# Feed-forward gate and up as seven block products, with weight sums by accumulating DMAs

## The chip, the cores and the metric

One Trainium2 chip, of which the kernel uses one core. The metric is the time of one execution on the device in microseconds (us).

## The reference

A sequence of 512 tokens with 1024 features goes through a network of two layers (one with a gated linear recurrence, one with stick-breaking attention), each followed by a feed-forward, and then through a second network with three kinds of attention, gates and an expert feed-forward. What is changed here is the first step of the two feed-forwards of the first network:

```python
def _rmsnorm(x, g):
    y = x32 * lax.rsqrt(jnp.mean(x32 * x32, axis=-1, keepdims=True) + RMS_EPS)
    return (y * g.astype(jnp.float32)).astype(x.dtype)
...
def _swiglu(h, w_gate, w_up, w_down):      # h = _rmsnorm(x, norm_ffn_g[layer])
    g = h @ w_gate.astype(h.dtype)
    u = h @ w_up.astype(h.dtype)
    return (jax.nn.silu(g) * u) @ w_down.astype(h.dtype)
```

w_gate and w_up have 1024 rows and 2816 columns, w_down the reverse.

## The kernel before

Activations lie transposed: X holds eight chunks c of 128 features (partitions) by 512 tokens. Every dense product is float32 work split into rounded parts: an operand is a high part in the rounded type fp32r and a low part, the rest, and the product is high x high, high x low and low x high, three matmuls for each tile of 128 x 128 weights (lines 2241 to 2243 in `pe_tiles`). The name WH, WL stands for a weight's high and low part, HH, HL for those of the normed input, MH, ML for those of the feed-forward's inner activation.

The whole kernel is one list of steps, written out once by `Order` and its callers; each engine's program walks over the same list and takes the steps that concern it, so the list is at once the order of each engine's queue. Engines wait for each other by semaphores. A weight *unit* is 128 output columns by up to eight k tiles (1024 elements for each partition). SP loads the units in order into six buffers RAW (line 1259), and reloads a buffer when DVE has made the low part of its last user (line 1249). Step `split` makes the parts: ACT rounds RAW to WH (line 1386), DVE subtracts to get WL (line 1712). There are three slots for parts; a unit is split two units ahead of its use, when the step of its matmuls is listed (line 125), and ACT waits until the slot's last user is through PE (line 1385).

In a feed-forward (`ffn_order`, line 331) the 2816 inner columns are 22 tiles f of 128, in two halves of eleven. For each f the list has gate's product (unit wg, eight k tiles, 24 matmuls of 512 columns), up's (wu, likewise), and the step `swiglu`: DVE scales both results from PSUM by the token scale RS (line 1722), ACT applies silu (1493), DVE multiplies (1844), ACT rounds the product to MH (1495), DVE makes ML (1716). After each half come eight down products of eleven k tiles (units of six and five) which DVE adds into X (`add_x`, line 1833). RS is 1/sqrt of the mean square; its steps (`rest`) come within the first tile's products, so that the norm's scale by token is applied to the results. The norm's scale by feature is applied ahead: step `high` rounds X times the gain to HH on ACT (1414) and squares X (1418), POOL adds up the squares (1369, 1372), step `low` makes HL on DVE (1752). At the entry of a feed-forward (norms 1 and 3) these steps follow each chunk of the output projection before it; the first tile's matmuls wait chunk by chunk.

## Time and profile before

| | |
|---|---|
| time, median of 3 executions | 2109.82 us (2109.67 to 2110.99) |
| span of the profiled execution, first to last instruction | 2108.2 us |
| clock granted to TensorE, mean | 0.999 |
| instructions | 24868 |
| moved by DMA | 352.09 MB, mean 167 GB/s |

The profile is of one execution; its span is 1.6 us under the median. No other time of that execution is given. A line of grouped instructions has the line of the kernel, the engine, the operation, output and inputs with their shape, the count, then busy time, mean duration and what the engine waited for before them. Durations of neighbouring instructions overlap, so the step between two starts is often shorter than one of them.

### The profile page before, as it was taken

Reading aid. Unit: us, or ns where it says so; the run is one execution under the profiler, and the core shown is the slowest. Engines: PE = TensorE matmul, PEld = TensorE weight load, DVE = VectorE, ACT = ScalarE, POOL = GpSimd, SP = SyncE. Lnnn points to the kernel's source line nnn. Section 1 sums busy time; section 2 is a strip of 40 time slices with the busy share of each in tenths; the row PEclk is TensorE's granted clock in tenths of the full one; section 3 lists DMA queues with packets and bytes.
Section 4 is the critical chain, followed back from the end, with each engine's and each line's share of the span. In section 5 each row is a group of like instructions: output and inputs, shape, how many; then the busy total and the mean of one; then the engine's idle time right before and its main releaser. Section 6 shows DMA issues by size and latency. Waiting matters only on the chain.

```text
span 2108.2 us, 24868 instructions
## 1 busy us (share of the span) xinstructions
PE 2082.8 (99%) x10137; PEld 1514.3 (72%) x10137; DVE 1022.5 (49%) x1516; ACT 749.7 (36%) x1076; POOL 143.7 (7%) x148
## 2 busy tenths in 40 slices
PE   9999999999999999999999999999999999999998
PEld 7878888888777788888888777777788534444433
DVE  7875433444666664434446656554564312122123
ACT  7774322323455543222333556433333110011012
POOL 0220000001000020000001010162100000000000
PEclk9999999999999999999999999999999999999999
DMA  5233223223211133233233322242236999999996
GB/s 220 76 104 110 86 81 124 98 72 116 76 61 60 61 108 100 72 119 102 76 95 111 115 67 72 60 94 73 68 110 247 392 426 427 427 427 426 427 427 273
DMA packets 89808, 352.09 MB, mean 167 GB/s; under 512 B 9568, under 2 KB 24160, under 8 KB 66144
## 3 DMA queue, kind: packets, MB, share of 16 engines
q1 hardware_dynamic: 84720, 342.48, 43.9%
q0 software_dynamic: 2192, 2.63, 1.0%
q10 hardware_dynamic: 2784, 5.41, 0.7%
q8 instruction: 81, 1.33, 0.3%
q14 instruction: 31, 0.25, 0.0%
HBM read 347.06 MB, written 2.10 MB: 166 GB/s over the span
## 4 chain that ended last, share of the span: by engine, by line
PE 87%; DMA 4%; DVE 4%; ACT 3%; issue 1%; POOL 0%; SPq 0%; ACTq 0%; DVEq 0%; POOLq 0%
PE PS L2241 20%; PE PS L2243 20%; PE PS L2242 20%; PE PS L2648 8%; PE PS L2690 4%; DMA SL<-in_wgu_dram 4%; PE PS L2284 2%; PE PS L2358 1%; PE PS L2632 1%; PE PS L2382 1%; PE PS L2372 1%; PE PS L2633 1%; DVE XC L1779 1%; PE PS L2480 1%; DVE WL L1712 1%
## 5 line engine op out<-in xcount | busy, mean ns | idle before, releaser
L2241 PE MATMUL PS<-HH,WH 128*128 128x512 f32 x1392 | 552.9, 397 | 0.8 <-DVE ACC L1942 0.6
L2243 PE MATMUL PS<-HH,WL 128*128 128x512 f32 x1392 | 542.5, 390 | 0.0
L2242 PE MATMUL PS<-HL,WH 128*128 128x512 f32 x1392 | 541.9, 389 | 0.0
L1712 DVE TENSOR_TENSOR WL<-RAW,WH 128x1024 fp32r<-128x1024 f32 (+4 forms) x302 | 344.1, 1141 | 290.2 <-ACT WH L1386 289.4
L1386 ACT ACTIVATE WH<-RAW 128x1024 fp32r<-128x1024 f32 (+4 forms) x302 | 286.2, 950 | 304.8 <-PE PS L2243 275.9
L2241 PEld LDWEIGHTS PS<-HH,WH 128*128 128x128 f32 x1392 | 261.3, 188 | 65.1 <-issue 10.3
L2243 PEld LDWEIGHTS PS<-HH,WL 128*128 128x128 f32 x1392 | 261.3, 188 | 55.6
L2242 PEld LDWEIGHTS PS<-HL,WH 128*128 128x128 f32 x1392 | 261.5, 188 | 53.2 <-issue 1.0
L2648 PE MATMUL PS<-SL,XS 128*64 128x512 f32 x928 | 220.8, 595 | 5.3 <-DMA SL<-in_wgu_dram 4.5
L2648 PEld LDWEIGHTS PS<-SL,XS 128*64 128x64 f32 x928 | 70.2, 137 | 134.0 <-issue 131.9
L2243 PE MATMUL PS<-MH,WL 128*128 128x512 f32 x352 | 136.9, 389 | 0.0
L2241 PE MATMUL PS<-MH,WH 128*128 128x512 f32 x352 | 136.9, 389 | 0.0
L2242 PE MATMUL PS<-ML,WH 128*128 128x512 f32 x352 | 136.9, 389 | 0.0
L1722 DVE TENSOR_TENSOR U<-PS,RS 128x512 f32<-128x512 f32 x44 | 30.4, 691 | 105.0 <-PE PS L2243 105.0
L1495 ACT ACTIVATE MH<-U 128x512 fp32r<-128x512 f32 x44 | 27.9, 633 | 140.0 <-DVE U L1844 140.0
L1661 ACT ACTIVATE HG<-PS 128x512 f32<-128x512 f32 x8 | 4.8, 596 | 204.1 <-PE PS L2648 204.1
L2242 PEld LDWEIGHTS PS<-ML,WH 128*128 128x128 f32 x352 | 66.1, 188 | 13.7
L2241 PEld LDWEIGHTS PS<-MH,WH 128*128 128x128 f32 x352 | 66.1, 188 | 13.7
L2243 PEld LDWEIGHTS PS<-MH,WL 128*128 128x128 f32 x352 | 66.1, 188 | 13.7
L2178 DVE TENSOR_SCALAR XS<-PS,V 128x256 f32<-128x256 f32 x32 | 17.4, 544 | 115.0 <-PE PS L2633 115.0
L1833 DVE TENSOR_TENSOR X<-X,PS 128x512 f32<-128x512 f32 x56 | 37.8, 684 | 55.9 <-PE PS L2243 55.9
L1369 POOL COPY SA<-SQ 128x512 f32<-128x512 f32 x4 | 2.7, 674 | 840.9 <-ACT SQ L1418 840.9
(376 smaller groups left out, 2734.3 us busy)
## 6 DMA issues: line engine op xcount, KB each, us to landing
SL<-in_wgu_dram SPq DMA_DIRECT2D x115, 1024.0 KB, 20.7
SL<-in_wdn_dram SPq DMA_DIRECT2D x52, 1024.0 KB, 23.2
RAW<-in_w_dram SPq DMA_DIRECT2D x46, 512.0 KB, 3.4
RAW<-in_wg_dram SPq DMA_DIRECT2D x44, 512.0 KB, 3.4
RAW<-in_wu_dram SPq DMA_DIRECT2D x44, 512.0 KB, 3.4
RAW<-in_wd_dram SPq DMA_DIRECT2D x32, 384.0 KB, 3.0
RAW<-in_wqkv_dram SPq DMA_DIRECT2D x24, 512.0 KB, 3.4
RAW<-in_wd_dram SPq DMA_DIRECT2D x32, 320.0 KB, 2.8
```

Of the source, the lines that this page charges most:

```text
L1386: e.activation(WH[u % NSPL][:, 0:n], RAW[raw_of[u]][:, 0:n], ACT.Copy).then_inc(*whs.did("u", u))
L1495: e.activation(MH[l][:, f, :], U1[l][:, z, :], ACT.Copy).then_inc(*hi.did("m", l, half, f))
L1712: e.tensor_tensor(wl, raw, wh.bitcast(F), ALU.subtract).then_inc(*wlo.did("u", u))
L1722: e.tensor_tensor(dst, src, r, ALU.mult).then_inc(*scaled.did(*event))
L1779: e.scalar_tensor_tensor(out=XC[s][:, :], in0=XB[p][:, 1 + j:T + 1 + j], scalar=vec("cw", 8 * j + c), in1=XC[s][:, :], op0=ALU.mult, op1=A ...
L1833: e.tensor_tensor(X[:, c, :], X[:, c, :], bank(*key), ALU.add).then_inc(*xup.did(*key))
L2241: e.matmul(out, wh[:, w], xh, start=k == 0, stop=False)
L2242: e.matmul(out, wh[:, w], xl, start=False, stop=False)
L2243: m = e.matmul(out, wl[:, w], xh, start=False, stop=k == g.total - 1)
L2284: m = e.transpose(bank(*key)[:, 128 * j:128 * j + 128], src, ident)
L2648: m = e.matmul(bank("h", i, n)[64 * e2:64 * e2 + 64, :], XS[:, k, x0:x0 + 64], SL[slot(l0 + e2)][:, 512 * n:512 * n + 512], start=k == 0, ...
L2690: m = e.matmul(bank("y", i, n)[64 * e2:64 * e2 + 64, :], HT[k // 2][:, 2 * (k % 2) + f, 64 * e2:64 * e2 + 64], SL[slot(l0 + e2)][:, 1024 * ...
```

## The change

With the input H (1024 features by 512 tokens) cut in two by features and by tokens, and the weights by rows of the contraction (first and last four k tiles) and by gate and up, the product of a tile f is a 2 x 2 block product. It is now made of seven products of 4 k tiles and 256 tokens, in Strassen's manner (Winograd's form), instead of eight: W11 and W21 are gate's two halves, W22 is up's last half, and T1, T2, T3, T4 are sums of weight blocks.

- Each of the seven is a unit "st" of 512 elements for each partition, with a split of its own into half a slot; three slots count as six halves, and units are split as far ahead as halves are free (`settle`, before: two units ahead). PE takes them in the order W11, T1, T2, W21, T3, W22, T4 (W21 earlier in a layer's first tile), with 84 matmuls of 256 columns a tile.
- Two PSUM banks, A and B, hold the partial results of a tile: products accumulate on top of each other, and at four points (`tap` a, b, c, d) ACT copies the value so far to SBUF before PE goes on adding.
- Sums of activation blocks are made once for each layer, at the entry (`differ` on POOL, `combine` and `combine_low` on ACT and DVE).
- Sums of weight blocks are made by DMA for each tile: SP loads a third buffer "e" with half of wu and half of wg (two DMAs of 256 KB); POOL issues four accumulating DMAs of 256 KB (`pool_sum`): T1 (up's first half, plus gate's first half from HBM), T3 (e, plus up's last half from HBM), T2 (e's other half, plus T3, after T3 has landed), T4 (gate's last half, plus T2, after T2 has landed and W21 has been split).
- The results of a tile are finished one tile later, in four steps between the next products (`silu_f`, `mul_f`, `high_f`, `low_f`). Only gate's result is scaled by RS before silu; up's is not, and the down results are scaled by RS instead, before they are added to X (one more DVE operation for each of 32 chunks).
- The split of the first feed-forward weights of layer 1 in two steps (`parted`, `awaited`) is dropped.

Its core:

```diff
@@ constants
+HALVES = 2 * NSPL
+W11, T1, T2, W21, T3, W22, T4 = range(7)
...
+    def settle(self):
+        self.pos, p = [], 0
+        for u in range(len(self.units)):
+            p += p % self.size(u)
+            self.pos.append(p)
+            p += self.size(u)
...
+            while v < len(self.units) and self.pos[v] + self.size(v) <= self.pos[s[1]] + HALVES:
+                self.split(v)
+                v += 1
+
+    def split(self, u):
+        if u + 2 < len(self.units) and self.units[u + 2][0] == "st" and self.units[u][0] != "st":
+            self.sums(*self.units[u + 2][1])
+        name, idx, _ = self.units[u]
+        if name != "st":
+            if u not in self.parted:
+                self.add("split_low" if u in self.rounded else "split", u)
+            return
+        self.add("split", u)
+        if idx[2] == W21:
+            self.add("sum", *idx[:2], T4)
+            if (idx[1] + 1) % FH:
+                self.sums(idx[0], idx[1] + 1, W11)
+
+    def sums(self, layer, i, j):
+        if j == W11:
+            for t in (T1, T3, T2):
+                self.add("sum", layer, i, t)
...
@@ add_x, normal
-    o.release(key, "xup", *key)
+    o.release(key, "scaled" if key[0] == "d" else "xup", *key)
+
+
+def normal(o, n, c):
+    o.add("high", n, c)
+    if n in (1, 3):
+        o.add("differ" if c < 4 else "combine", n, c % 4)
+    o.add("low", n, c)
+    if n in (1, 3) and c > 3:
+        o.add("combine_low", n, c % 4)
...
@@ ffn_order
...
+            u = [o.unit("st", (layer, i, j), 4) for j in range(7)][0]
...
+            ahead(W11)
+            product(W11)
+            if f:
+                o.add("output_a", layer, i - 1)
+                o.release(("A", layer, i - 1), "scaled", "a", layer, i - 1)
             if i == 0:
+                product(W21, 0, 3)
+                ahead(T1)
+                product(T1, 0, 3)
+                tap("a")
+                ahead(T2)
+                product(T2, 0, 3)
+                ahead(W21)
+                product(W21, 3, 4)
+                product(T1, 3, 4)
+                tap("d")
+                product(T2, 3, 4)
+                tap("b")
+                ahead(W22)
+                product(W22)
+                ahead(T3)
+                product(T3)
                 rest(o, norm - 1)
-            o.tiles(("u", layer, i), k, 8)
-            o.add("swiglu", layer, half, f)
-            o.release(("g", layer, i), "scaled", "g", layer, i)
-            o.release(("u", layer, i), "scaled", "u", layer, i)
+                tap("c")
+            else:
+                tap("a")
+                ahead(T1)
+                product(T1)
+                late("silu_f")
+                tap("d")
+                ahead(T2)
+                product(T2)
+                late("mul_f")
+                tap("b")
+                ahead(W21)
+                product(W21)
+                late("high_f")
+                ahead(T3)
+                product(T3)
+                late("low_f")
+                tap("c")
+                ahead(W22)
+                product(W22)
+            ahead(T4)
+            product(T4)
+            o.add("output_b", layer, i)
+            o.release(("B", layer, i), "scaled", "b", layer, i)
+        o.add("output_a", layer, i)
+        o.release(("A", layer, i), "scaled", "a", layer, i)
+        for what in ("silu_f", "mul_f", "high_f", "low_f"):
+            o.add(what, layer, half, f)
         for c in range(DC):
             key = ("d", layer, half, c)
             o.lin(key, [("wd", (layer, half, c, slice(None), slice(0, 6)), 6),
                         ("wd", (layer, half, c, slice(None), slice(6, 11)), 5)], ("m", layer, half), fresh=c == 0)
             add_x(o, key, c)
             if half == 1:
-                o.add("high", norm, c)
-                o.add("low", norm, c)
+                normal(o, norm, c)
...
@@ slots of RAW and of WH, WL
+        fetch, fetch_of = [], {}
+        for u, (name, idx, nt) in enumerate(units):
+            if u == o.late:
+                late_fetch = len(fetch)
+            if name != "st":
+                fetch_of[u] = len(fetch)
+                fetch.append((u, name, idx, nt, u))
+            elif idx[2] == W11:
+                l, i, _ = idx
+                for m, name, last in (("g", "wg", T4), ("u", "wu", W22), ("e", None, T4)):
+                    fetch_of[m, l, i] = len(fetch)
+                    fetch.append(((m, l, i), name, (l, i), 8, u + last))
+        raw_of = {f[0]: n % NRAW if n < late_fetch else (n - late_fetch) % NLATE for n, f in enumerate(fetch)}
...
+        def weights(l, i, which):
+            m, x = {W11: ("g", 0), W21: ("g", 1), T4: ("g", 1), T1: ("u", 0), W22: ("u", 1), T3: ("e", 0), T2: ("e", 1)}[which]
+            return RAW[raw_of[m, l, i]][:, 512 * x:512 * x + 512]
...
@@ sp_program
+                if before_in[n] is not None:
+                    e.wait_ge(*wlo("u", before_in[n]))
+                if name is None:
+                    _, l, i = u
+                    for t, m in ((T3, "wu"), (T2, "wg")):
+                        e.dma_start(weights(l, i, t).rearrange("p (a b) -> p a b", a=4), I[m][l, i][:, 0:4]).then_inc(
+                            *d_raw[raw_of[u]].did(*u, *(() if t == T2 else (t,))))
+                    continue
...
@@ pool_program
+                elif kind == "differ":
+                    n, m = a
+                    x_ready(e, n, m)
+                    e.tensor_tensor(S1[n // 2][:, m // 2, 256 * (m % 2):256 * (m % 2) + 256], X[:, m, 0:256], X[:, m, 256:512],
+                                    ALU.subtract).then_inc(*differ.did(n, m))
+                elif kind == "sum":
+                    pool_sum(e, *a)
...
+        def pool_sum(e, l, i, which):
+            u, dst = o.first_unit[l, i], weights(l, i, which)
+            if which in (T1, T3):
+                m = ("u" if which == T1 else "e", l, i)
+                e.wait_ge(*d_raw[raw_of[m]](*m))
+                src = I["wg"][l, i][:, 0:4] if which == T1 else I["wu"][l, i][:, 4:8]
+                e.dma_start(dst.rearrange("p (a b) -> p a b", a=4), src, accum_op=ALU.add).then_inc(
+                    *d_sum[which].did(l, i))
+            elif which == T2:
+                e.wait_ge(*d_sum[T3](l, i))
+                e.dma_start(dst, weights(l, i, T3), accum_op=ALU.add).then_inc(*d_sum[which].did(l, i))
+            else:
+                e.wait_ge(*d_sum[T2](l, i))
+                e.wait_ge(*wlo("u", u + W21))
+                e.dma_start(dst, weights(l, i, T2), accum_op=ALU.add).then_inc(*d_sum[which].did(l, i))
...
@@ act_split
...
+            name, idx, nt = units[u]
+            n = nt * 128
+            if name != "st":
+                e.wait_ge(*d_raw[raw_of[u]](u))
+            elif idx[2] in (W11, W21, W22):
+                m = ("u" if idx[2] == W22 else "g", *idx[:2])
+                e.wait_ge(*d_raw[raw_of[m]](*m))
+            else:
+                e.wait_ge(*d_sum[idx[2]](*idx[:2]))
+            for v in held[u]:
+                e.wait_ge(*lin("u", v))
+            e.activation(split_slot(WH, u)[:, 0:n], unscaled(u), ACT.Copy).then_inc(*whs.did("u", u))
...
@@ act_program
...
+                elif kind == "tap":
+                    l, i, t = a
+                    z = i % 2
+                    if i == 0:
+                        e.wait_ge(*lo("s", 1 + 2 * l, 3))
+                    e.wait_ge(*lin("u", o.first_unit[l, i] + {"a": W11, "d": T1, "b": T2, "c": T3}[t]))
+                    dst = {"a": G1[l][:, z, 0:256], "d": S1[l][:, z, 0:256], "b": U1[l][:, z, 0:256],
+                           "c": U1[l][:, z, 256:512]}[t]
+                    e.activation(dst, bank("B" if t == "d" else "A", l, i)[:, 0:256], ACT.Copy).then_inc(*kept.did(t, l, i))
...
@@ dve_program
+                    c, l, (name, i) = m + 4, n // 2, NORMS[n]
...
+                    e.tensor_scalar(x22, X[:, c, 256:512], gc, None, ALU.mult).then_inc(*comb.did("x22", n, m))
+                    e.wait_ge(*comb("x22", n, m))
+                    e.scalar_tensor_tensor(out=n5, in0=X[:, m, 256:512], scalar=gm, in1=x22, op0=ALU.mult,
+                                           op1=ALU.subtract).then_inc(*comb.did("n5", n, m))
+                    e.wait_ge(*comb("n5", n, m))
+                    e.scalar_tensor_tensor(out=m2, in0=X[:, m, 0:256], scalar=NG[l][:, m:m + 1], in1=n5, op0=ALU.mult,
+                                           op1=ALU.add).then_inc(*comb.did("m2", n, m))
+                    e.wait_ge(*comb("m2", n, m))
+                    e.scalar_tensor_tensor(out=n3, in0=X[:, c, 0:256], scalar=gc, in1=m2, op0=ALU.mult,
+                                           op1=ALU.add).then_inc(*comb.did("n3", n, m))
+                elif kind == "combine_low":
+                    n, m = a
+                    l, (name, i) = n // 2, NORMS[n]
...
+                    if key[0] == "d":
+                        _, l, half, _ = key
+                        if c or half:
+                            e.wait_ge(*xup("d", l, half if c else 0, (c - 1) % DC))
+                        e.tensor_tensor(ST[:, :], bank(*key), RS[:, :], ALU.mult).then_inc(*scaled.did(*key))
+                        e.wait_ge(*scaled(*key))
+                        e.tensor_tensor(X[:, c, :], X[:, c, :], ST[:, :], ALU.add).then_inc(*xup.did(*key))
...
-                elif kind == "swiglu":
+                elif kind == "mul_f":
                     l, half, f = a
...
+                    i = half * FH + f
+                    U = U1[l][:, i % 2, :]
                     e.wait_ge(*silu("f", l, i))
...
+                    e.wait_ge(*comb("r22", l, i))
+                    e.tensor_tensor(U, U, S1[l][:, i % 2, :], ALU.mult).then_inc(*mul.did("f", l, i))
+                elif kind == "low_f":
+                    l, half, f = a
+                    i = half * FH + f
+                    dve_low(e, ML[l][:, f, :], U1[l][:, i % 2, :], MH[l][:, f, :], "m", l, half, f)
+                elif kind == "output_b":
+                    l, i = a
+                    G, U, P = (t[l][:, i % 2, :] for t in (G1, U1, S1))
+                    e.wait_ge(*kept("c", l, i))
+                    e.tensor_tensor(U[:, 256:512], P[:, 0:256], U[:, 256:512], ALU.subtract).then_inc(*comb.did("r22", l, i))
+                    e.wait_ge(*lin("u", o.first_unit[l, i] + W22))
+                    e.tensor_tensor(G[:, 0:256], bank("B", l, i)[:, 256:512], G[:, 0:256], ALU.add).then_inc(
+                        *comb.did("r11", l, i))
+                    e.tensor_tensor(U[:, 0:256], bank("B", l, i)[:, 0:256], U[:, 0:256], ALU.subtract).then_inc(
+                        *scaled.did("b", l, i))
+                    e.wait_ge(*comb("r11", l, i))
+                    e.tensor_tensor(G[:, 0:256], G[:, 0:256], RS[:, 0:256], ALU.mult).then_inc(*comb.did("g", l, i))
+                elif kind == "output_a":
+                    l, i = a
+                    e.wait_ge(*lin("u", o.first_unit[l, i] + T4))
+                    e.tensor_tensor(G1[l][:, i % 2, 256:512], bank("A", l, i)[:, 0:256], RS[:, 256:512], ALU.mult).then_inc(
+                        *scaled.did("a", l, i))
...
@@ pe_product
+        def pe_product(e, l, i, j, k0, k1):
+            n, u = 1 + 2 * l, o.first_unit[l, i] + j
+            b, x = ("B", int(j == W21)) if j in (T1, W21, W22) else ("A", 0)
+            out = bank(b, l, i)[:, 256 * x:256 * x + 256]
+            opens = j in (W11, T1) if i else j in (W11, W21)
+            after = {T2: "a", T3: "b", T4: "c", W22: "d", W21: "d" if i else None}.get(j)
+            wh, wl = split_slot(WH, u), split_slot(WL, u)
+            if k0 == 0:
+                e.wait_ge(*wlo("u", u))
+                if opens and o.before[b, l, i]:
+                    e.wait_ge(*freed(b, l, i))
+                if after:
+                    e.wait_ge(*kept(after, l, i))
+            for k in range(k0, k1):
+                if i == 0:
+                    e.wait_ge(*(lo("h", n, k) if j == W11 else lo("h", n, 4 + k) if j in (W21, T4) else lo("s", n, k)))
+                if j in (T1, T2, T3):
+                    s = {T1: 0, T2: 1, T3: 2}[j]
+                    xh, xl = SH[l][:, k, s, :], SO[l][:, k, s, :]
+                else:
+                    c, t = {W11: (k, 0), W22: (k, 256), W21: (4 + k, 0), T4: (4 + k, 256)}[j]
+                    xh, xl = HH[:, c, t:t + 256], HL[:, c, t:t + 256]
+                w = slice(128 * k, 128 * k + 128)
+                e.matmul(out, wh[:, w], xh, start=opens and k == 0, stop=False, skip_group_check=True)
+                e.matmul(out, wh[:, w], xl, start=False, stop=False, skip_group_check=True)
+                m = e.matmul(out, wl[:, w], xh, start=False, stop=k == 3, skip_group_check=True)
+                if k == 3:
+                    m.then_inc(*lin.did("u", u))
```

## Rows read from the trace of the kernel before

**Rows 1.** The page: busy us (share) by engine, granted clock and GB/s in 40 slices
```profile
PE 2082.8 (99%) x10137; PEld 1514.3 (72%) x10137; DVE 1022.5 (49%) x1516; ACT 749.7 (36%) x1076; POOL 143.7 (7%) x148
...
PEclk9999999999999999999999999999999999999999
...
GB/s 220 76 104 110 86 81 124 98 72 116 76 61 60 61 108 100 72 119 102 76 95 111 115 67 72 60 94 73 68 110 247 392 426 427 427 427 426 427 427 273
```

**Rows 2.** The page: the chain that ended last, shares of the span by line
```profile
PE PS L2241 20%; PE PS L2243 20%; PE PS L2242 20%; PE PS L2648 8%; PE PS L2690 4%; DMA SL<-in_wgu_dram 4%; PE PS L2284 2%; PE PS L2358 1%; PE PS L2632 1%; PE PS L2382 1%; PE PS L2372 1%; PE PS L2633 1%; DVE XC L1779 1%; PE PS L2480 1%; DVE WL L1712 1%
```

**Rows 3.** Timeline, PE, gate and up of layer 0: start, us, engine, line, operation
```profile
220.21 0.39 PE L2241 MATMUL PS<-HH,WH 128*128 128x512 f32 x1
...
231.09 0.39 PE L2241 MATMUL PS<-HH,WH 128*128 128x512 f32 x1
```

**Rows 4.** Timeline, PE, first and after the last of 24 matmuls of 256 columns
```profile
1141.23 0.28 PE L2241 MATMUL PS<-YP,WH 128*128 128x256 f32 x1
...
1144.10 0.40 PE L2241 MATMUL PS<-HH,WH 128*128 128x512 f32 x1
```

**Rows 5.** Groups of DVE and ACT by form, busy us, mean ns
```profile
L1712 DVE TENSOR_TENSOR WL<-RAW,WH 128x512 fp32r<-128x512 f32 x26 | 18.3, 705 | 15.7 <-ACT WH L1386 15.5
...
L1716 DVE TENSOR_TENSOR YP<-AT,YP 128x256 fp32r<-128x256 f32 x8 | 2.8, 420 | 0.0
...
L1386 ACT ACTIVATE WH<-RAW 128x512 fp32r<-128x512 f32 x26 | 16.1, 619 | 2.9 <-PE PS L2243 2.9
...
L1397 ACT ACTIVATE PT<-PS 128x256 f32<-128x256 f32 x16 | 6.0, 376 | 5.4 <-PE PS L2284 4.6 <-issue 0.7
```

**Rows 6.** Timeline, ACT and DVE: neighbouring starts
```profile
233.42 0.63 ACT L1495 ACTIVATE MH<-U 128x512 fp32r<-128x512 f32 x1 [3.25 <-DVE U L1844]
233.96 1.04 ACT L1386 ACTIVATE WH<-RAW 128x1024 fp32r<-128x1024 f32 x1
...
1135.62 2.56 ACT L1516 ACTIVATE YP<-AT 128x256 fp32r<-128x256 f32 x8
...
1139.83 2.43 DVE L1716 TENSOR_TENSOR YP<-AT,YP 128x256 fp32r<-128x256 f32 x7
```

**Rows 7.** DMA issues: count, KB each, median us to landing
```profile
RAW<-in_wg_dram SPq DMA_DIRECT2D x44, 512.0 KB, 3.4
...
RAW<-in_wbr_dram SPq DMA_DIRECT2D x24, 256.0 KB, 2.6
...
AT<-in_mem_dram POOLq DMA_DIRECT2D x1, 1024.0 KB, 5.2
...
SQ<-VZ ACTq DMA_DIRECT2D x10, 128.0 KB, 2.0
```

**Rows 8.** Groups of POOL by form: its own DMA issues, mean ns
```profile
L1337 POOL DMA_DIRECT2D BI<-in_rpb_dram x64 | 33.7, 535 | 221.9 <-PE PS L2431 115.7 <-PE PS L2480 105.6 <-POOL BM L1349 0.6
...
L1324 POOL DMA_DIRECT2D AT<-in_mem_dram x1 | 0.7, 734 | 0.0
```

**Rows 9.** Windows, gate and up of layer 0: busy, clock, DMA share, GB/s
```profile
185.00:285.00 100.00, 100.00 (x443) 82.81 (x442) 46.58 (x56) 29.57 (x37) 0.00 (x0) 1.00 0.29 92
```

**Rows 10.** Timeline, DVE, a chunk at the entry of layer 0's feed-forward
```profile
165.91 1.52 DVE L1712 TENSOR_TENSOR WL<-RAW,WH 128x1024 fp32r<-128x1024 f32 x1 [0.72 <-ACT WH L1386]
167.36 0.67 DVE L1833 TENSOR_TENSOR X<-X,PS 128x512 f32<-128x512 f32 x1
168.83 0.75 DVE L1752 SCALAR_TENSOR_TENSOR HL<-X,V,HH 128x512 fp32r<-128x512 f32 x1 [0.79 <-ACT HH L1414]
170.29 1.52 DVE L1712 TENSOR_TENSOR WL<-RAW,WH 128x1024 fp32r<-128x1024 f32 x1 [0.72 <-ACT WH L1386]
```

**Rows 11.** Windows, around the one stretch at the lower clock
```profile
1634.00:1638.40 4.40, 2.62 (x29) 2.02 (x29) 2.50 (x12) 3.77 (x5) 0.71 (x1) 1.00 1.01 425
1638.40:1641.80 3.40, 3.40 (x9) 2.63 (x9) 3.18 (x11) 1.37 (x2) 3.40 (x2) 0.50 1.02 424
1641.80:1646.00 4.20, 4.20 (x20) 3.39 (x19) 3.73 (x13) 0.00 (x0) 0.60 (x1) 1.00 1.01 419
```

164 lines of the change are left out of this document (107 added, 57 removed).

## The prediction

> **What bounds the kernel now.** I read the busy times first: PE is at 99% of the span at the full clock, DVE at 49% [rows 1]. The chain that ended last confirms that this is no average over an idle machine: three fifths of it are the three matmul lines of the split product (20% each), 2241 to 2243 [rows 2]. So time goes only by taking matmul time away, and comes by making PE wait. A matmul's own duration is no price, since matmuls overlap; the step from start to start is. In gate and up, two starts 48 matmuls apart lie 10.88 us apart, 0.2267 us for 512 columns [rows 3]. That 10.88 us is one frame, an f tile of gate and up; there are 44, eleven in each half of each layer. For 256 columns with a weight load each, the change's own form, 24 starts take 2.87 us, 0.1196 us each [rows 4]: 53% of the wide one, not 50%.
>
> **What the products save.** A frame becomes 7 products x 4 k tiles x 3 = 84 narrow matmuls, 84 x 0.1196 = 10.05 us, and a product is 1.435 us. That is 0.83 us less a frame, 36.5 us in all, or 110.5 against 119.7 us for the eleven frames of a half. This is all that the change can win, 1.7%. Everything else asks whether PE can be fed at that pace.
>
> **DVE and ACT.** DVE gives up two scalings of 512 and two splits of 1024 a frame and takes seven splits of 512, five operations of 256, and keeps the product with silu and its low part. Steps come from neighbouring starts: a split of 512 lasts 0.705 us and the next starts some 0.08 before its end, so 0.62; 256 columns take (2.43 - 0.42) / 6 = 0.34 [rows 5, 6]. 7 x 0.62 + 5 x 0.34 + 2 x 0.62 = 7.3 us of 10.05. ACT: a step of 512 is 0.54 (233.42 to 233.96), of 256 0.31, from PSUM 0.38 [rows 5, 6]: 9 x 0.54 + 4 x 0.38 = 6.4 us. Neither fills the frame; PE hides both, and if that cover goes they have 2.7 and 3.6 us left. Both queues are in order, though, and now stand behind DMAs.
>
> **The sums by DMA: the step that decides.** Four accumulating DMAs of 256 KB a frame are issued by POOL, in the order T4 of frame f, then T1, T3, T2 of f+1. T4's waits for DVE's split of W21 of f (it overwrites that weight). T2's waits for T3's to land, with nothing behind it but the next frame's. ACT's split of T2 of f+1 waits for T2's sum; behind it in ACT's queue are the tap of T3 and the split of W21, and that split releases T4's next sum. So there is a ring: issue T4, issue T1, T3 until landed, T2 until landed, splits of T2 and W21, again. PE isn't in it, and no run-ahead of the splits shortens it.
> - Issue: POOL's one large DMA took it 0.73 us, its small ones 0.54 [rows 8]. I take 0.73, so T4 and T1 put 1.5 us ahead of T3 (bounds 1.1 and, with twice the descriptors, 2.9).
> - Landing: no row has an accumulating DMA. A plain 256 KB takes 2.6 us, 512 KB 3.4: 1.8 us and 0.8 for each 256 KB; from POOL 1024 KB took 5.2 where this line gives 5.0, so POOL adds 0.2. A transfer from SBUF to SBUF took 2.0 at 128 KB, where the line has 2.2, so that the source is in SBUF gains little [rows 7]. Lower bound, a sum is a plain copy: 2.8 us. Upper, it reads both terms and writes one in turn, like 768 KB: 4.4. I take both reads, like 512 KB: 3.6, since an addition must fetch its destination too.
> - T4, T1 and T3 leave POOL 0.73 us apart, but 512 KB at the best rate of the page, 427 GB/s, is 1.23 us of the 16 engines [rows 1]. T3 is thus late by 2 x 0.5 = 1.0 us (0 if a sum is a plain copy, 2.2 at the upper bound).
> - Tail: ACT's split of T2, 0.62; DVE's low of T2 and then of the feed-forward tile, 1.23 more, longer than ACT's tap and its split of W21 beside them; DVE's low of W21, 0.70; 0.15 for the handovers: 2.7.
>
> Ring: 1.5 + 3.6 + 1.0 + 3.6 + 2.7 = 12.4 us, against 10.05 for PE. The Trainium skill ("Collectives: The Full Stack", on the bandwidth ceiling) says that a reduce in the DMA engine costs no time for the add but reads two sources, and so runs at half the rate of a copy. By this rule the sum is the forecast; by the copy's price it is the first rival; no trace here shows it yet.
>
> Besides the ring, W21's product waits (through a tap behind ACT's split of T4) for T4's sum: 3.6 + 0.62 + 0.54 + 0.38 after its issue. With the products of W21 and T3 (2.9), T3's tap (0.4), ACT's and DVE's split of W21 (1.3) and the handovers that is 9.9 us a frame, under both.
>
> The loads also grow, from 1 to 1.5 MB a frame, and the sums read 2 MB more. Now 92 GB/s keep the engines at 0.29 [rows 9]; 1.57 MB at 427 GB/s are 3.7 us, the four sums 4.9: 8.6 of 12.4 us. Loads and T2's sum meet in the ring: 0 to 1.2 us more. I take 0, since T2 is a quarter of what is in flight.
>
> **A half by the ring.** The first sum of T4 is issued 1.9 us before the half's first matmul (its split belongs to the last down unit before). The eleventh comes 10 rings later; then 3.6 + 1.5 us to W21, and W21, T3, W22, T4: 5.7. Length: -1.9 + 124 + 3.6 + 1.5 + 5.7 = 132.9 us against 119.7, so +13.2, and +53 in four halves.
>
> **Entry into each feed-forward.** For chunks 4 to 7 the combinations add on DVE, besides the addition into X (0.67), the low part (0.75) and the weights (1.52), which leave it idle a third of the 4.38 us of a chunk [rows 10], four operations of 256 that wait for each other (0.43 each) and low parts of 256, 512, 256. DVE then needs 0.7 + 1.5 + 3.7 = 5.9 us for a chunk, 1.5 late on each of three: 4.5 us, which T4's first sum (behind them in DVE's queue) inherits. Twice: +9. Bounds: +4 (the first four k tiles of W11, W21, T1, T2 give 4.7 us of cover) and +20 (another 5 us each for the last chain and the 3.35 us reciprocal behind it). POOL's subtraction and its sums of squares share its queue with the first frame's sums; these have a dozen us. The second operation on each down output adds 0.7 us to DVE per 7.5 us chunk, hidden behind the next eleven k tiles; at the stage's end the next stage's first k tiles hide it. The down split's changed run-ahead, by halves of a slot, and the split of the last output weights in one step cost nothing: the same depth for wide units, hidden by PE.
>
> **Sum.** 2108.2 + 53 + 9 = 2170. The median shown, 2109.8, is 1.6 above that execution's span: 2172.
>
> **Rivals.**
> 1. *Sums as cheap as copies.* Ring: 1.5 + 2.8 + 2.8 + 2.7 = 9.8 us, under PE's 10.05: each half falls by 9.2, entries cost 9: -28, **2082**. For it: enough engine time is idle, and SBUF as a source costs nothing. Against: the second read. It decides from a ring of 10.86 us, where 4 x (108.6 + 8.9 - 119.7) + 9 = 0; below it the kernel is faster. Chance 0.2, and 0.2 for rings of 10.3 to 11.6 us (2087 to 2140), which lie on both sides (0.07 faster, 0.05 same, 0.08 slower).
> 2. *Sums dearer still*, three passes in turn: 4.4 to land, T3 late by 2 x (1.84 - 0.73) = 2.2; ring 15.2, half 161.7, **2287**. For it: the copies' line shows nothing of a read that must precede its write. Chance 0.15, with all that lies above 2240.
> 3. *The clock.* In the forecast PE idles 2.3 us a frame. In one stretch of 4.4 us it worked 2.62 us, and then ran at 0.50 for 3.4 us, that is at 1.2 GHz; the next stretch was at 2.4 again [rows 11]. Such a fall in each frame costs 1.7 us of PE's work; with it the loop through PE is 11.6, still under 12.4, so it is covered. If the clock stayed low, a frame would be 20.1 us and the end at 2500. The skill ("TensorE: Matmul & The Clock Gate", its rules for kernels) warns of idle gaps between bursts. Chance 0.03.
> 4. *Not what it says*: a narrow matmul held by its 0.188 us weight load would make the frame 15.8 us. Rows 4 have the same pair at 0.1196, so hardly: 0.01. DVE's order of waits, not its load, stalling PE by a us a frame: **2125**, 0.03.
>
> **How the numbers follow.** The forecast's case (rings of 11.6 to 13.2) has 0.38, the likeliest single one, with its own range 2140 to 2205. Faster: 0.2 + 0.07 = 0.27; within 0.2%, 4 us, about what can be told from no change here: 0.05; slower 0.68. The range goes down to 2080, where all of the saving comes and entries cost little more than their bound, and up to 2260; some 0.08 lies below and 0.12 above.
>
> **What would show it.** Narrow matmuls 0.12 us apart in a product; starts of W11's product 12.4 us apart and not 10.05; PE's idle time before the product of W21 or T2's weights, ended by DVE's WL or ACT's tap; ACT's split idle until a DMA into RAW; sums landing 3.6 us after issue, T3's 4.6. If they land at 2.8, or the frame is 10.05, the forecast is wrong and rival 1 holds; if ACT waits for PE or DVE in its splits and not for a DMA, the ring isn't what decides.

## The result and the profile after

The changed kernel takes 2416.84 us (median of 4 executions, 2411.13 to 2419.61) against 2109.89 us of the kernel before beside it (2109.67 to 2110.99): the ratio is 1.145, with a 95% interval of 1.1434 to 1.1467. It is slower, as forecast, but by 307 us where 62 were predicted, and the time lies outside the range. The page of the changed kernel, busy time by engine, granted clock and GB/s [rows 1 before]:

```profile
span 2409.1 us, 29692 instructions
...
PE 2141.6 (89%) x11721; PEld 1644.9 (68%) x11721; DVE 1180.7 (49%) x1958; ACT 897.6 (37%) x1496; POOL 303.3 (13%) x332
...
PEclk9998789887999997889987999999999999999999
...
GB/s 195 94 92 166 137 152 119 153 148 128 114 95 62 60 77 95 142 153 128 137 153 138 138 103 131 59 74 73 84 66 90 234 356 427 426 427 426 427 427 294
```

PE's busy time has grown, not shrunk, although its products are fewer: matmuls at the lower clock last longer, and the clock dips in just the slices of gate and up. DVE's share stays at 49%, ACT's is 37% (36% before). The chain that ended last, shares by line [rows 2 before]:

```profile
DMA RAW<-RAW 11%; PE PS L2497 11%; DMA RAW<-in_wu_dram 10%; PE PS L2499 10%; PE PS L2498 10%; PE PS L2935 8%; PE PS L2977 4%; DVE WL L1906 3%; DMA SL<-in_wgu_dram 2%; PE PS L2569 2%; POOL RAW L1527 1%; ACT WH L1556 1%; PE PS L2531 1%; PE PS L2533 1%; PE PS L2532 1%
```

A fifth of the span, more than the whole loss, is now waiting for two kinds of DMA: a sum from SBUF to SBUF (T2's) and one from HBM (T3's). On PE's own timeline the four halves of gate and up last 191.2, 192.8, 205.8 and 188.5 us (before 120.7, 119.9, 120.8, 119.9): 297 us more, of 300.9 by which the span of this profiled execution is longer (it ran in 2411.1 us, 5.7 under the median). A down half is 60.0 us and the first stage of attention 187.0 us, as before. So the loss is nearly all in gate and up, where a frame, from one `output_a` on DVE to the next, has a median of 17.6 us in place of 10.88 [rows 3]; most are between 16.5 and 19. The chain of two frames in layer 0 (start us, us, what):

```profile
262.58 0.86 POOL RAW L1527
263.45 0.21 POOL RAW L1519
263.65 6.13 DMA RAW<-in_wu_dram
269.78 0.28 issue
270.07 6.73 DMA RAW<-RAW
...
276.82 0.64 ACT WH L1556
...
277.48 0.69 DVE WL L1906
278.18 0.60 DVE ML L1910
278.78 0.61 DVE WL L1906
...
279.94 0.86 POOL RAW L1527
...
281.02 7.04 DMA RAW<-in_wu_dram
...
288.34 5.82 DMA RAW<-RAW
```

This is the predicted ring, step by step in its order: T4's and T1's issue, T3 until landed, T2 until landed, ACT's split of T2, DVE's low parts of T2, of the feed-forward tile and of W21, and T4 again, 17.36 us later. PE is nowhere in it. It only shows the end of the ring's wait: its product of W21 waits 5.2 us for tap c, which stands in ACT's queue behind T2's split, and then runs at half clock (a granted clock of 0.50 from 276 to 280 us), 0.214 us from start to start (timeline, PE, of the changed kernel):

```profile
277.87 0.55 PE L2531 MATMUL PS<-HH,WH 128*128 128x256 f32 x1 [5.22 <-ACT U L1609]
278.22 0.41 PE L2532 MATMUL PS<-HL,WH 128*128 128x256 f32 x1
278.43 0.41 PE L2533 MATMUL PS<-HH,WL 128*128 128x256 f32 x1
```

Gate and up of layer 0 as in [rows 9] (busy of PE, PEld, DVE, ACT, POOL, granted clock, DMA share, GB/s); the DMA engines are busy 0.64 of the time in place of 0.29:

```profile
185.00:285.00 100.00, 70.68 (x482) 68.66 (x481) 45.81 (x81) 39.90 (x78) 21.40 (x24) 0.81 0.64 148
```

The DMA view of 262 to 282 us: packets, MB and share of 16 engines by queue (q0 is POOL's, q1 SP's), then the issues with their time to landing:

```profile
q0 software_dynamic: 639, 1.18, 34.9%
q1 hardware_dynamic: 576, 1.57, 22.1%
...
RAW<-RAW POOLq DMA_DIRECT2D x3, 256.0 KB, 3.2
RAW<-in_wg_dram POOLq DMA_DIRECT2D x2, 256.0 KB, 5.8
RAW<-in_wu_dram POOLq DMA_DIRECT2D x2, 256.0 KB, 6.6
RAW<-in_wg_dram SPq DMA_DIRECT2D x1, 512.0 KB, 5.1
RAW<-in_wu_dram SPq DMA_DIRECT2D x1, 512.0 KB, 6.2
```

T4's sum, issued first, lands in 3.2 us; T1's takes 5.8, T3's 6.6. The loads, 3.4 us before [rows 7], are slower too. POOL's queue moved less than SP's and held the engines longer: 1.18 MB in 0.349 x 20 us is 169 GB/s, SP's 1.57 MB 355 GB/s. SP's four loads of a later frame are issued at 267.2 to 268.6 us, while T3's sum is still under way and just before T2's:

```profile
267.22 0.33 SPq L1401 DMA_DIRECT2D RAW<-in_wg_dram  x1
...
268.59 0.48 SPq L1389 DMA_DIRECT2D RAW<-in_wg_dram  x1
```

They wait for DVE's low part of T4 (266.50 to 267.19), and so for T4's sum, which lands at 265.8. The mean share of 0.64 hides this: from 264 to 274 us the DMA engines are busy 0.91 of the time and more.

### The profile page after: what moved, and what is told of

Read it like the earlier page. It is cut to its first block, busy times and chain, and to the rows that moved or that the text cites. A ratio compares the mean times of both kernels' runs of the same rounds, so it can differ in the third digit from the quotient of the medians.

```text
span 2409.1 us, 29692 instructions
## 1 busy us (share of the span) xinstructions
PE 2141.6 (89%) x11721; PEld 1644.9 (68%) x11721; DVE 1180.7 (49%) x1958; ACT 897.6 (37%) x1496; POOL 303.3 (13%) x332
## 3 DMA queue, kind: packets, MB, share of 16 engines
q0 software_dynamic: 27536, 48.77, 12.5%
## 4 chain that ended last, share of the span: by engine, by line
PE 59%; DMA 24%; DVE 8%; ACT 3%; issue 3%; POOL 2%; ACTq 0%; SPq 0%; POOLq 0%; DVEq 0%
DMA RAW<-RAW 11%; PE PS L2497 11%; DMA RAW<-in_wu_dram 10%; PE PS L2499 10%; PE PS L2498 10%; PE PS L2935 8%; PE PS L2977 4%; DVE WL L1906 3%; DMA SL<-in_wgu_dram 2%; PE PS L2569 2%; POOL RAW L1527 1%; ACT WH L1556 1%; PE PS L2531 1%; PE PS L2533 1%; PE PS L2532 1%
## 5 line engine op out<-in xcount | busy, mean ns | idle before, releaser
L1906 DVE TENSOR_TENSOR WL<-RAW,WH 128x512 fp32r<-128x512 f32 (+4 forms) x522 | 448.1, 868 | 570.6 <-ACT WH L1556 568.0
L1556 ACT ACTIVATE WH<-RAW 128x512 fp32r<-128x512 f32 (+4 forms) x522 | 380.8, 741 | 566.6 <-DMA RAW<-RAW 272.9
L2531 PE MATMUL PS<-HH,WH 128*128 128x256 f32 x704 | 240.6, 342 | 236.1 <-ACT U L1609 203.2
L2497 PE MATMUL PS<-HH,WH 128*128 128x512 f32 x688 | 278.4, 405 | 1.5 <-DVE WL L1906 0.6
L2499 PE MATMUL PS<-HH,WL 128*128 128x512 f32 x688 | 268.7, 391 | 0.0
L2498 PE MATMUL PS<-HL,WH 128*128 128x512 f32 x688 | 268.1, 390 | 0.0
L2532 PE MATMUL PS<-HL,WH 128*128 128x256 f32 x704 | 232.7, 331 | 0.0
L2533 PE MATMUL PS<-HH,WL 128*128 128x256 f32 x704 | 231.7, 329 | 0.0
L2531 PE MATMUL PS<-SH,WH 128*128 128x256 f32 x528 | 152.9, 290 | 7.4 <-issue 6.4
L2532 PE MATMUL PS<-SO,WH 128*128 128x256 f32 x528 | 151.9, 288 | 0.0
```

Of the source, the lines that this page charges most:

```text
L1556: e.activation(split_slot(WH, u)[:, 0:n], unscaled(u), ACT.Copy).then_inc(*whs.did("u", u))
L1906: e.tensor_tensor(wl, unscaled(u), wh.bitcast(F), ALU.subtract).then_inc(*wlo.did("u", u))
L2497: e.matmul(out, wh[:, w], xh, start=k == 0, stop=False)
L2498: e.matmul(out, wh[:, w], xl, start=False, stop=False)
L2499: m = e.matmul(out, wl[:, w], xh, start=False, stop=k == g.total - 1)
L2531: e.matmul(out, wh[:, w], xh, start=opens and k == 0, stop=False, skip_group_check=True)
```

## The experiments

Frames are given from one `output_a` on DVE to the next, without the first and last of a half, which are often shorter; halves are from PE's timeline. Times are medians; the kernel before, measured beside e1 to e4, e5 to e8 and e9 to e12, took 2109.4, 2110.0 and 2110.4 us. Ratios are to these.

**e1: no sums.** The four sums are left out; the splits read the weights as loaded.

```diff
@@ sums, split
-            for t in (T1, T3, T2):
-                self.add("sum", layer, i, t)
+            pass
...
-            self.add("sum", *idx[:2], T4)
```

> The four accumulating DMAs of a frame and all waits for them are left out (T1 to T4 use the unsummed weights; everything else, the loads into e too, stays). Ring theory (the ring T4's sum, T3's, T2's, splits sets the 17.4 us frame): the frame falls to PE's 10.05 us, and what is left over 2073 us is the price of the entries: 2080 to 2095 us. Rival, the in-order queues of ACT and DVE hold PE even with the sums gone: frames of 11 us and more, 2125 us or more. Clock theory (PE is slow since its clock falls): says nothing else than the first, as the gaps go with the sums.

Measured: 2117.59 us, ratio 1.0035 (1.0024 to 1.0046). Frames are 10.08 us, as the ring theory has it, and the time lies between the two that were expected; halves are 128.4, 111.0, 136.1 and 111.0. So the sums are 299 of the 307 us, and the products' saving is what was predicted: 111.0 us in the halves without an entry, against 110.5. But the two entries take 17.4 and 25.1 us more than that, 42.5 instead of 9, and eat the whole saving of 36 us. PE's timeline has its gaps there: 5.6 us for DVE's WL at 175.0 in layer 0, then 1.8, 1.3, 2.2 and 1.1, with half clock between 175 and 184 us. DVE's timeline has a part of the cause (e7 tests how much), one chunk of layer 0's entry:

```profile
161.43 0.68 DVE L2066 TENSOR_TENSOR X<-X,PS 128x512 f32<-128x512 f32 x1
...
163.58 1.47 DVE L1965 SCALAR_TENSOR_TENSOR U<-X,V,G 128x256 f32<-128x256 f32 x1
164.97 0.74 DVE L1943 SCALAR_TENSOR_TENSOR HL<-X,V,HH 128x512 fp32r<-128x512 f32 x1
...
168.16 0.68 DVE L2066 TENSOR_TENSOR X<-X,PS 128x512 f32<-128x512 f32 x1
```

6.7 us a chunk, not the 5.9 predicted or the 4.38 of before [rows 10]. One operation of the four takes 1.47 us in place of 0.48: POOL's sum of squares for the norm runs beside it (1.29 us, at 163.47).

**e2: sums made by POOL.** All four as additions in SBUF, no third load.

```diff
@@ pool_sum
-                e.dma_start(dst, weights(l, i, T2), accum_op=ALU.add).then_inc(
+                e.tensor_tensor(dst, dst, weights(l, i, T2), ALU.add).then_inc(
```

> All results are computed. The sums are made by POOL with four tensor_tensor of 512 a frame (T3, T1, T2, T4) instead of by DMA, and SP no longer loads e. Ring theory: the ring becomes 4 x 1.34 us and the tail of 3.1, 8.5 us, under PE's 10.05, so 2080 to 2100 us, faster than before. Rival: POOL and DVE hinder each other (DVE's split of 1024 took 1.52 us instead of 1.23 beside POOL's additions before), POOL's 5.4 and DVE's 7.3 us of a frame lie end to end, frame 12.5 us, 2180 us.

Measured: 2251.81 us, ratio 1.0671 (1.0655 to 1.0687), frames of 12.8 and 14.2. Both expected times are missed, the rival's by 72 us. Half of the loss is gone, but a new one has come: DVE is busy 1307.7 us, where it was 1181.0 in e1. e8 shows how such additions lengthen DVE's operations.

**e3: copies in place of sums.** `accum_op=ALU.add` dropped from all four; the values are those of the source, silu's scale is 0.

> The four DMAs of POOL stay, with their sizes, sources, order and waits, but copy instead of adding; silu is applied to zero times its input, so that the feed-forwards add nothing. Ring theory: what is dear is the sharing of the engines with SP's loads and with each other more than the addition: T3 lands after about 5 us, T2 after 5 to 6, ring 15, about 2310 us. Rival, the addition itself is what is dear: both land after 3 us, ring 11 to 12, 2130 to 2170 us.

Measured: 2255.53 us, one run, frames of 12 to 16. The chain of one frame:

```profile
270.86 0.54 POOL RAW L1527
271.39 0.52 POOL RAW L1519
271.91 3.76 DMA RAW<-in_wu_dram
...
275.96 7.02 DMA RAW<-RAW
```

The time is between the two expected ones, and each is right about one landing. T3's copy lands in 3.8 us, where its sum takes 6.1 to 7.0. T2's, a plain copy of 256 KB, takes nearly as long as its sum: 7.0 us here, a median of 5.7 over the 44 frames against 6.7. So most of T2's landing isn't the addition's price. The page gives the price in engine time: POOL's queue has 6.7% of 2253.7 us x 16 engines; less what it has without sums (1.0% of 2116.0) that is 130 us for 176 copies, 0.74 us each. In the changed kernel it is 12.5% of 2409.1 less the same, 280 us: **1.6 us of all 16 engines for a sum**, twice a copy and more.

**e4: loads held until T2's sum has landed.**

```diff
@@ sp_program
+                if isinstance(u, tuple) and u[0] == "g" and u[2] % FH:
+                    e.wait_ge(*d_sum[T2](u[1], u[2] - 1))
```

> All results are computed. SP holds the loads of the frame after next until T2's sum for the next frame has landed, so that T2's sum no longer meets them. Ring theory: T2 lands 3.3 us after its issue instead of 6.3, ring 14.3 us, about 2290 us, unless the loads, now 3 us later, are met by T3 or hold it up: then the ring stays at 17 and T3's landing or POOL's wait for the e loads is longer by what T2 gained. Rival, the addition from SBUF to SBUF is slow by itself: T2 stays above 5.5 us.

Measured: 2321.37 us, one run, frames of 15.0 to 15.8 for the most part. The chain:

```profile
266.14 5.20 DMA RAW<-in_wg_dram
271.34 0.28 issue
271.62 4.84 DMA RAW<-in_wu_dram
276.47 0.28 issue
276.75 3.22 DMA RAW<-RAW
```

T2's sum lands in 3.2 us, as fast as T4's: its other 2.6 to 3.5 us in the changed kernel are SP's loads beside it. The chain is another one, though: load of the third buffer, T3, T2, next load, 15.2 us with no engine in it but SP, which issues the loads.

**e5: T2's sum not behind T3's.** It adds up's second half, which lies in SBUF.

```diff
@@ pool_sum
-                e.wait_ge(*d_sum[T3](l, i))
-                e.dma_start(dst, weights(l, i, T3), accum_op=ALU.add)
+                e.dma_start(dst, weights(l, i, W22), accum_op=ALU.add)
```

> T2's sum adds up's second half, which lies in SBUF, in place of T3, and is issued right behind T3's without waiting for it; silu's scale is 0, so that the wrong weights stay finite. Instructions and bytes are the same (the source of one 256 KB sum is another SBUF buffer). Theory (the two sums in a row, T3's 6.1 to 7.0 us and T2's 5.8 to 6.7, are the frame): one of the two goes out of the chain, and what is left is 17.4 - 6.4 = 11.0 us, up to 12.5 because the three sums now share the engines: 44 frames x 5 to 6.4 us off 2416.8, that is 2135 to 2200 us. Rival (the traffic itself is too much for the DMA engines, in whatever order): the frame stays above 15 us, 2330 us or more.

Measured: 2230.27 us, ratio 1.0571 (1.055 to 1.0592), frames of 11.8 to 14.0. The same instructions and bytes, 187 us less: most of the loss is the two landings in a row, not the traffic. It is 30 us above the expected band, because the one landing left in the chain takes 7.8 to 8.8 us with the other sums and the loads beside it.

**e6: loads of the third buffer cut to 8 elements for each partition.**

```diff
@@ sp_program
-                        e.dma_start(weights(l, i, t).rearrange("p (a b) -> p a b", a=4), I[m][l, i][:, 0:4]).then_inc(
+                        e.dma_start(weights(l, i, t)[:, 0:8], I[m][l, i][:, 0, 0:8]).then_inc(
```

> SP's two loads of the third buffer are cut from 512 to 8 elements for each partition (the rest of the buffer is old data, silu's scale is 0); all four sums and their waits stay. What goes is 0.5 MB of loads a frame, the part of the loads that the change added. Theory (landing is long because the sums meet SP's loads): a third of what T2's sum meets is gone, so of the 3.0 us by which it lands later than T4's (3.2 us, nothing beside it) one goes, and of T3's likewise: frame 15.4, 2330 us; T1's and T3's median fall from 5.4 and 6.4. Rival (a sum's landing is long for itself, by its HBM source or its queue): frame within 0.5 us of 17.4, 2395 us or more.

Measured: 2369.17 us, ratio 1.1229, frames of 15.0 to 17.9. T2's sum lands in 4.6 to 6.2 us (6.7 and 5.8 in the changed kernel; medians of 44 frames 5.3 and 6.7), T3's still in 6.1 to 7.1. Between the two theories: those loads cost about 1 us of the frame, half of what I expected, and only in T2's landing. T3's is not lengthened by them.

**e7: e1 without the combinations.** The four chained DVE operations for each of chunks 4 to 7 are left out as well.

```diff
@@ dve_program, combine
-                    e.tensor_scalar(x22, X[:, c, 256:512], gc, None, ALU.mult).then_inc(*comb.did("x22", n, m))
...
-                    e.scalar_tensor_tensor(out=n3, in0=X[:, c, 0:256], scalar=gc, in1=m2, op0=ALU.mult,
-                                           op1=ALU.add).then_inc(*comb.did("n3", n, m))
```

> The kernel without sums (e1), and at the two entries the four chained DVE operations of 256 columns for each of four chunks are left out too (x22, n5, m2, n3): ACT and the low parts read X itself, so the same number and widths of ACT copies and DVE low parts remain, and products with the right time but wrong operands. e1 had halves of 128.4, 111.0, 136.1, 111.0 us, so its two entries cost 42.5 us. Theory (DVE's queue at the entry makes PE late, then behind it the last chain): 4 x 0.43 = 1.7 us less for each of four chunks, 6.9 for an entry, and the two gaps behind the last chunk, 5.6 and 1.8 us, go with it for the most part: 10 to 12 us an entry, 2117.6 - 22 = 2096 us, which would be faster than the kernel before. Rival (the entry is long by the reciprocal of 3.35 us, the order of the first products and the clock, and not by the combinations): 3 us or less an entry, 2112 us or more.

Measured: 2104.80 us, ratio 0.9976 (0.9967 to 0.9985). The first halves are 122.9 and 128.8 us, so the entries fall from 42.5 to 29.7 us: 13 us, between theory (22) and rival (under 6). A chunk still takes 5.8 us for the operations X, HL, SO, HL, WL: 1.7 us of operations are gone, but DVE now waits 0.86 us of each chunk for ACT's HH. This is the changed kernel's work with free sums and half its combinations, and it gains 0.24%.

**e8: T3 and T2 by POOL, T1 and T4 by DMA.** The third buffer isn't loaded.

```diff
@@ pool_sum
+                if which == T3:
+                    e.tensor_tensor(dst, weights(l, i, T1), weights(l, i, W22), ALU.add)
+                else:
+                    e.dma_start(dst, weights(l, i, W11), accum_op=ALU.add)
...
+                e.tensor_tensor(dst, weights(l, i, W11), weights(l, i, T3), ALU.add)
```

> All values as in the changed kernel. T3's and T2's sums, the two that stand in a row in the chain, are additions on POOL (1.5 us each by e2), T1's and T4's are accumulating DMAs from SBUF to SBUF; the third buffer isn't loaded. Theory (two DMA landings in a row made the frame, and e2 was held by four POOL additions that stretch DVE's operations beside them): ring = T4's issue 0.5, T3 1.6, T1's issue 0.5, T2 1.5, tail 3.3 = 7.4 us, under PE's 10.05; DVE is stretched half as long as in e2, so frames of 10.3 to 11.5 us: 2117.6 + 44 x 0.2 to 1.4 = 2127 to 2180 us. Rival (any sum beside the splits costs the same, wherever it is made): as e2, 2240 to 2255 us.

Measured: 2231.39 us, ratio 1.0588 (1.0568 to 1.0608), frames of 10.7, 12.6 and 14.1. A miss: in the frames of 12.6 and 14.1 us no DMA is in the chain any more, and yet they are far from 10.05. One cause is in DVE's timeline:

```profile
239.06 1.93 DVE L2092 TENSOR_TENSOR U<-S,U 128x256 f32<-128x256 f32 x1
...
241.58 2.15 DVE L2099 TENSOR_TENSOR G<-G,RS 128x256 f32<-128x256 f32 x1
```

and, at the same times, in POOL's:

```profile
239.11 1.59 POOL L1521 TENSOR_TENSOR RAW<-RAW 128x512 f32<-128x512 f32 x1
...
241.85 1.59 POOL L1526 TENSOR_TENSOR RAW<-RAW 128x512 f32<-128x512 f32 x1
```

The other is in ACT's:

```profile
244.70 0.63 ACT L1687 ACTIVATE S<-G 128x512 f32<-128x512 f32 x1 [2.32 <-DVE G L2103]
245.24 0.37 ACT L1612 ACTIVATE S<-PS 128x256 f32<-128x256 f32 x1
```

Both operations of DVE, 0.41 us otherwise, start within 0.3 us of a POOL addition and end 0.2 to 0.3 us after it. `output_a` comes late by both; silu waits 2.3 us for it, and tap d, which PE waits for, stands behind silu.

**e9: the sums in another order.** T3 and T1 of tile f+1 go ahead of T4 of tile f, with semaphores of their own for odd and even tiles.

```diff
@@ split
-            self.add("sum", *idx[:2], T4)
-            if (idx[1] + 1) % FH:
-                self.sums(idx[0], idx[1] + 1, W11)
+            if more:
+                self.add("sum", idx[0], idx[1] + 1, T3)
+                self.add("sum", idx[0], idx[1] + 1, T1)
+            self.add("sum", *idx[:2], T4)
+            if more:
+                self.add("sum", idx[0], idx[1] + 1, T2)
```

> All values as in the changed kernel, the same four sums and loads; only the order in POOL's queue differs: T3 and T1 of tile f+1 go ahead of T4 of tile f (before: T4 of f, then T1, T3, T2 of f+1), and each sum has a semaphore for odd and one for even tiles. Theory (the frame is the chain T4's issue, T3's landing, T2's landing, splits): T3's landing goes out of it, and what is left is T4's issue 0.5, T2's issue and landing 0.5 + 3.2 and 1.6 for T4's sum ahead of it, 0 to 2 for the loads, tail 3.3: 9.1 to 11.1 us. But the engines have 4 x 1.6 us for the sums (12.5% of 2409 us less 1.0% of 2108, over 176 sums) and 1.5 MB of loads at 355 GB/s, 4.4 us, in a frame: 10.8. Frame 11 to 13 as in e5, 2155 to 2245 us. Rival (the traffic or a sum's own length, not the order): within 1.5 us of 17.4, 2350 us or more.

Measured: 2324.20 us, ratio 1.1011 (1.0994 to 1.1027), frames of 13.8 to 18.2. A gain of 93 us, and 80 us short of the band. The chain has closed in another way:

```profile
260.64 4.79 DMA RAW<-in_wg_dram
...
265.71 0.45 POOL RAW L1523
...
266.25 0.54 POOL RAW L1523
266.78 6.39 DMA RAW<-RAW
...
275.17 0.70 DVE WL L1910
...
275.91 5.73 DMA RAW<-in_wg_dram
```

T3's sum waits in POOL's queue for the load of its buffer, that load for DVE's split of an earlier T4, and T4's sum now stands behind T3's. I had priced the landings on the new path and not what the moved instruction waits for. The run has a number for T3 all the same: issued first, with no load in flight, its sum lands in 4.3 us here, 4.0 in the median.

**e10: e9 with T2 on POOL**, gate's half not loaded again, and tap d ahead of silu.

```diff
@@ pool_sum
-                e.dma_start(dst, weights(l, i, T3), accum_op=ALU.add)
+                e.tensor_tensor(dst, weights(l, i, W11), weights(l, i, T3), ALU.add)
```

> e9, and besides: T2's sum is one addition on POOL (gate's first half plus T3, both in SBUF), so SP doesn't load gate's first half a second time; the tap d stands ahead of silu in ACT's queue. All values as in the changed kernel. Theory: the engines have 3 x 1.6 + 1.25 MB at 355 GB/s, 3.5, that is 8.3 us a frame; the ring is T4's issue 0.5, POOL 1.6, tail 3.3 = 5.4; DVE has 7.3 us and is blocked 1.6 by POOL's one addition, 8.9; so nothing but PE is left at 10.05: frames 10.1 to 11.3, 2118 to 2172 us. Rival (several smaller waits of the in-order queues stay, whichever sum is made where): frames above 12, 2200 us or more.

Measured: 2295.04 us, ratio 1.0881 (1.0863 to 1.0899). The same miss: in most frames its chain is e9's, load 4.7, two issues, T4's sum 6.3 us, with T2's addition not in it; in some it goes through ACT's and DVE's queues instead of the load (243 to 253 us). I can't say what each of the three edits gave of the 29 us against e9.

**e11: T1's sum left out.**

```diff
@@ sums
-            for t in (T1, T3, T2):
+            for t in (T3, T2):
```

> The changed kernel with T1's sum left out (T1's product takes up's first half as it is; silu's scale is 0); T4, T3 and T2 as they were. T1's sum is not waited for in the chain, it only stands between T4's and T3's in the queue. Theory (a sum holds the 16 engines for 1.6 us, and T3 lands behind T4's and T1's): the frame loses the issue, 0.54, and 1.6: 17.4 - 2.1 = 15.3 us, 2417 - 92 = 2325 us. Rival (T3's 6 to 7 us are its own, since it reads from HBM or from a busy queue): only the issue goes, frame 16.9, 2393 us.

Measured: 2368.03 us, ratio 1.1222 (1.1187 to 1.1257), midway. The chain:

```profile
270.38 0.54 POOL RAW L1527
270.91 5.07 DMA RAW<-in_wu_dram
...
276.27 8.02 DMA RAW<-RAW
```

T3 lands in 4.8 to 5.1 us instead of 6.1 to 7.0, the 1.6 us of one sum, as expected. But T2's sum takes 7.5 to 9.0 us instead of 5.8 to 6.7: it is issued 0.5 us after the first of SP's loads (276.27 and 275.77) where it was 2.9 us after it, and meets all of them. Half of what the one landing and the issue give, the other landing takes. The clock was lower than in the changed kernel (0.901 against 0.937) and the time shorter, so the clock isn't what decides. It does cost something: behind the last down half the same work took 992.4 us at 0.95 in place of 980.6 at 1.00, and the other execution, at 0.947 over the whole, took 2361.78 us.

**e12: e8 with tap d ahead of silu.**

```diff
@@ ffn_order
-                late("silu_f")
                 tap("d")
+                late("silu_f")
```

> e8 with one step moved: tap d stands ahead of silu in ACT's queue. All values as in the changed kernel. Theory (in e8 two POOL additions block DVE's operations beside them, 1.93 and 2.15 us in place of 0.41; so output_a is late, silu waits 2.3 us for it, and the tap, which PE waits for, stands behind silu; the idle PE then runs at 0.5): PE no longer waits for output_a; DVE has 7.3 + 1.5 + 1.75 = 10.6 us a frame, so frames of 10.6 to 11.5, 2142 to 2181 us. Rival (DVE's blocked time reaches PE by the weights' splits as well): frames stay above 12.5, 2215 us or more.

Measured: 2149.17 us, ratio 1.0182 (1.0167 to 1.0198), frames of 10.36 for the most part (9.3 to 12.4, once 14.2), as expected: one line moved is 82 us. So DVE's stretched operations cost PE their time in e8 through the tap; the stretch itself is still there (DVE is busy 1262.0 us, 1181.0 in e1). A DMA sum is back in the chain, with 5% of the span. It is the fastest version with all values right, 268 us better than the changed kernel, and still slower than the kernel before: its second halves are 117.0 and 116.2 us (before 119.9), its first ones 136.2 and 144.7.

No version here beats the kernel before with all its arithmetic. With four halves of e12's 117 us and entries that cost nothing one would have some 13 us, 0.6%. To get there the first tile of a layer would have to be an ordinary one, so that the combinations are made beside it; that wasn't tried.

## Why the prediction was wrong, point by point

- **What the products save: right.** 10.08 us a frame and 111.0 us a half (e1) against 10.05 and 110.5. The step of 0.1196 us from [rows 4] held; rival 4's held matmul didn't occur.
- **The ring: right as a mechanism.** Its steps stand in the chain in the predicted order, with PE outside, and e5, which takes one landing out without changing a byte count, gives back 187 us.
- **The ring's size: the step that failed.** 17.4 us, not 12.4: the landings of T2 and T3 were priced too low. The ten rings of a half, from its first T4 sum to its eleventh, take 171.4, 181.3, 186.3 and 177.9 us, not 124: 221 of the 245 us that were missed. By terms, in the two frames shown: issue 1.1 (predicted 1.5; POOL needs 0.54 for each); T3 6.1 to 7.0 (4.6); T2 5.8 to 6.7 (3.6); tail 3.1, and 0.3 between the two landings (2.7). Over 44 frames the medians are 6.4 for T3 and 6.7 for T2, and T2 ranges from 3.2 to 8.3.
  - *T2, loads beside its sum: "I take 0".* This is the largest error, 3 us a ring, well over the bound of 1.2. The reason given was that T2 is a quarter of what is in flight. Beside 1.5 MB of SP's loads its sum takes 2.6 to 3.5 us more than without them (3.2, e4), and a mere copy also (5.7 in the median, e3, where T4's copy takes 2.2). The ring makes them meet in every frame: T4's sum is its first step, and T4's split, as soon as that sum has landed, lets the loads start, three us ahead of T2's. A mean engine share of 0.64 says nothing against it. Why a neighbour lengthens one transfer by that much is not shown.
  - *T3, late by 1.0 behind T4's and T1's.* Of a sum with its source in SBUF the landing was over-priced: 3.2 us alone (e8, e4), not 3.6. T3's comes from HBM and was under-priced: 4.0 us issued first (e9), 4.9 behind one sum (e11), 6.4 behind two. So two sums ahead cost it 2.4 us, not 1.0. Their engine time was under-priced, 1.6 us and not 1.23, and I had added only what exceeded POOL's issue steps, and at 427 GB/s; POOL's queue moves 169 while it sums.
  - The rule on reduces, that they run at half the rate of a copy (the Trainium skill, "Collectives: The Full Stack", on the bandwidth ceiling), fits in engine time: 1.6 us against 0.74. It speaks of rate; what decided here was what is in flight beside a sum.
- **Rival 1** (sums as cheap as copies) falls twice: they aren't, and e3 shows that copies in this order take 2256 us, not 2082. **Rival 2** named three passes in turn and 2287 us; a single sum is cheaper than it says, yet the ring is longer than its 15.2. The time lies in its share of 0.15, but not for its reason: like the forecast it priced T2's sum without the loads beside it.
- **Rival 3, the clock: as told, covered.** The frame shown has the fall after PE's 5.2 us of idle time, but PE isn't in the ring; e11 is faster than the changed kernel at a lower clock. Once the DMAs are out of the way it counts: in e8 PE runs the first products after its wait at 0.214 us a step. That step is also less than twice 0.1196, so a frame wholly at the lower clock would be 84 x 0.214 = 18.0 us, not 20.1, as an estimate.
- **DVE and ACT** at 7.3 and 6.4 us a frame filled nothing, right: in e1's second half they are busy 7.4 and 6.5 us a frame. **The order of waits in the queues** (in the prediction DVE's) had 0.03 and a us a frame; it shows as soon as the sums leave the DMA (e8 to e12: 2 us a frame from one tap behind silu in ACT's queue).
- **Entries: wrong**, 42.5 us for 9, above the bound of 20. That is e1's number, and of the 245 us it explains little: in the changed kernel the first T4 sum of a layer comes 7.8 us after the half's first matmul, where 2.6 was predicted (1.9 ahead, and 4.5 late), and the rings that follow cover the rest. Three terms in e1: 6.7 us a chunk and not 5.9, of which 1.0 is the operation stretched by POOL; no wait of PE for DVE was counted behind the last chunk, where 5.6 us stand in the trace; and the first products, cut in parts to cover the norm, have gaps of 1 to 2 us between them. e7 gives 13 us to the four chained operations; how the other 30 divide was not tested.
- **Down's second operation and the rest at nothing: right,** the down halves are 60.0 us in both kernels. Outside the four halves the profiled execution loses 4 us: 1.9 before the first of them (167.5 for 165.6), 2.7 before the third, and 1.1 fewer behind the last down half.

## What to carry to other kernels

Price a transfer in a loop by what is in flight with it in that very phase, not by its share of the mean: a loop brings the same neighbours together each time round. Before moving an instruction in an in-order queue, write down what it waits for and which loop that closes; e9 and e10 missed for that alone, and 82 us were a tap behind a silu. And ask first what the idea gains if everything it adds were free: that was 36 us here, and the two entries alone took 42.5.
